# Expert stages: most token tiles dense on TensorE, the rest fetched row by row on VectorE

## The reference

```python
def block(hb):                       # 128 tokens
    q = (hb @ wq).reshape(n, 8, 2, 128)
    s = jnp.einsum('thpk,hpnk->thpn', q, keys)
    s1, i1 = lax.top_k(s[:, :, 0], 16)
    s2, i2 = lax.top_k(s[:, :, 1], 16)
    cand = (s1[..., :, None] + s2[..., None, :]).reshape(n, 8, 256)
    cidx = (i1[..., :, None] * 128 + i2[..., None, :]).reshape(n, 8, 256)
    sc, pos = lax.top_k(cand, 16)
    eidx = jnp.take_along_axis(cidx, pos, axis=-1)
    gw = jax.nn.softmax(sc, axis=-1)
    a = jnp.einsum('thkd,td->thk', u_tab[eidx], hb)
    w = gelu(a) * gw
    return jnp.einsum('thk,thkd->td', w, v_tab[eidx])
```

## Time and profile before

| | us |
|---|---|
| median of 3 runs | 5842.98 (5840.63 to 5846.96) |
| profiled execution, its own time | 5849.18 |
| its span, first to last instruction | 5847.3 |
| expert stage of layer 0 (from 1142.6 to 3329.3) | 2186.7 |
| expert stage of layer 1 (from 4334.9 to 5812.0) | 1477.1 |
| DVE busy | 4668.5 |
| PE busy | 1702.9 |

### The profile page before, as it was taken

One profiled execution on the slowest core, in us unless ns is written; L12 is line 12 of the kernel. 1 busy time (PEld: TensorE's weight loads), 2 busy tenths in 40 slices (PEclk: granted clock), 3 DMA queues, 4 the chain that ended last, 5 costly groups with the idle time before them and its releaser, 6 DMA issues. The chain is left out here.

```text
span 5847.3 us, 35407 instructions
## 1 busy us (share of the span) xinstructions
PE 1702.9 (29%) x9845; PEld 1288.3 (22%) x9845; DVE 4668.5 (80%) x7565; ACT 706.3 (12%) x993; POOL 2711.6 (46%) x2768
## 2 busy tenths in 40 slices
PE   6976888700000000000000087577750000000001
PEld 5844876600000000000000054333540000000001
DVE  3156753299999999999999925799339999999998
ACT  2134222100000000000000114444210000000000
POOL 0001320055676676767777400254006667677764
PEclk8987988855555555555555588888875555555555
DMA  4111012178999999999999710111219899999996
GB/s 153 51 59 62 5 30 80 66 312 316 358 407 387 365 406 345 409 370 375 409 410 409 283 39 1 39 47 44 78 67 366 321 355 410 368 376 409 409 410 279
DMA packets 477618, 1473.74 MB, mean 252 GB/s; under 512 B 55510, under 2 KB 124876, under 8 KB 474860
## 3 DMA queue, kind: packets, MB, share of 16 engines
q0 software_dynamic: 368640, 1342.34, 59.0%
q1 hardware_dynamic: 104336, 120.65, 6.3%
q10 hardware_dynamic: 4444, 8.48, 0.4%
HBM read 1458.72 MB, written 12.58 MB: 252 GB/s over the span
## 5 line engine op out<-in xcount | busy, mean ns | idle before, releaser
L1436 POOL DMA_INDIRECT rows<-peer_u,expert x1280 | 1224.0, 956 | 1261.7 <-DVE expert L1583 707.2
L1638 DVE SCALAR_TENSOR_TENSOR banks<-rows,weight,banks 128x1024 f32<-128x1024 f32 x1260 | 1534.8, 1285 | 5.8 <-DMA rows<-peer_v,expert 5.7
L1632 DVE CUSTOM_DVE_ANT_0 junk<-rows,banks 128x1024 f32<-128x1024 f32 x1280 | 1497.8, 1220 | 30.9 <-DMA rows<-peer_u,expert 18.4
L1436 POOL DMA_INDIRECT rows<-peer_v,expert x1280 | 1208.1, 944 | 461.1 <-issue 228.9
L1457 PE MATMUL banks<-ident,y_tok 128*128 128x128 f32 x80 | 19.7, 427 | 3088.8 <-DVE y_tok L1601 3088.8
L1457 PEld LDWEIGHTS banks<-ident,y_tok 128*128 128x128 f32 x80 | 15.7, 223 | 3091.5 <-DVE y_tok L1601 3091.5
L2169 POOL TENSOR_TENSOR prods<-s,cos 128x512 f32<-128x512 f32 x64 | 81.0, 1265 | 607.2 <-DVEq L2154 607.2
L1009 POOL TENSOR_TENSOR z<-expo,keep_k 128x384 f32<-128x384 f32 x28 | 30.8, 1107 | 606.5 <-ACT expo L985 606.5
L1483 ACT COPY y_tok<-banks 128x1024 f32<-128x1024 f32 x10 | 10.1, 1012 | 1576.7 <-DVEq L1654 1576.7
L1450 PE MATMUL banks<-ident_r,h_hi 128*128 128x128 f32 x80 | 33.6, 420 | 528.5 <-DVEq L1654 515.3
L1473 ACT ACTIVATE gate<-gate 128x128 f32<-128x128 f32 x10 | 3.1, 310 | 1342.0 <-DVE gate L1561 1342.0
(11 more groups left out here) (378 smaller groups left out, 5409.4 us busy)
## 6 DMA issues: line engine op xcount, KB each, us to landing
rows<-peer_u,expert POOLq DMA_INDIRECT x1280, 9.4
rows<-peer_v,expert POOLq DMA_INDIRECT x1280, 10.1
peer_wq_in<-peer_wq SPq DMA_DIRECT2D x16, 1024.0 KB, 5.3
ada_ring<-ada_w SPq DMA_DIRECT2D x32, 512.0 KB, 3.8
y_t<-ev_w_in SPq DMA_DIRECT2D x12, 1024.0 KB, 5.3
ada_ring<-ada_w SPq DMA_DIRECT2D x6, 2048.0 KB, 8.0
scores<-score_out SPq DMA_DIRECT2D x10, 1024.0 KB, 3.9
score<-scores SPq DMA_DIRECT2D x10, 1024.0 KB, 7.9
```

Source lines behind the costliest of these rows:

```text
L1436: pool.indirect_dma_start(out=ring[:, at % RING, :], out_offset=None, in_=tables[kind == "v"], in_offset=bass.IndirectOffsetOnAxis(ap=expe ...
L1632: last = nc.vector.tensor_tensor_reduce(out=junk[:, s % 2], in0=row, in1=tile_h(t), scale=1.0, scalar=0.0, op0=ALU.mult, op1=ALU.add, accu ...
L1638: last = nc.vector.scalar_tensor_tensor(out=acc(s % 2), in0=row, scalar=weight[:, t, s:s + 1], in1=acc(s % 2), op0=ALU.mult, op1=ALU.add)
```

## The change

The expert stage becomes two stages, and each token tile is now of one of two kinds. Layer 0 has four dense tiles and two fetched ones, layer 1 three and one (`DENSE_TILES`).

For **dense tiles** all 16384 experts are evaluated. `stage_peer_activate` goes over 128 expert tiles of 128 rows of `peer_u` (expert = 128 a + b; tile b holds the rows with the same b, so a partition reads 4 KB at a stride of 512 KB). For each, ACT makes the high part `u_hi` (`round_u`), POOL the low part `u_lo` (`low`), PE turns both by 16 transposes in two halves, ACT copies the turned halves out of PSUM (`turned_out`), PE makes 24 products of 512 (layer 1: 384) token columns, ACT applies gelu, and SP stores the result in HBM (`activations`). The gates of a dense tile become a table in HBM as well: for four tokens at a time (`quad`) DVE makes one-hot matrices (`one_hots`: one 128x512 comparison and four 128x128 operations), PE multiplies them, ACT copies the result (`keep`). `stage_peer_mix` reads `peer_v`, the activations and the gate table back, in 32 groups of 4 expert tiles: DVE multiplies activations by gates (`multiply`), ACT and DVE split the product (`w_hi`, `low`), ACT and POOL split `v` (`v_hi`, `v_lo`), and PE sums 12 products for each of 8 channel blocks; DVE adds each to the residual (`add`).

For **fetched tiles** nothing changes in kind: 256 fetches and dot products in the first stage of layer 0 and 256 fetches and weighted sums in the second (layer 1: 128 and 128), now with a ring of 8. They and the routing are spread over the expert tiles by a table of row numbers (class `Turns`, whose constants set the expert tile in which a gate event stands in the lists of PE, ACT and SP, and in which POOL fetches). The score stage also stores the residual in HBM (3 MB), since its room in SBUF is used for the routing, and the second stage loads it again. The total of fetches falls from 2560 to 768; 256 MB of tables are read in order.

```diff
+RING = 8
+DENSE_TILES = (4, 3)
...
+            self.events.setdefault(min(self.expert_tile(row) + 1, KEYS), []).append((kind, i))
...
+    def us(self, row):
+        steps = min(max(row, 0), (len(self.order) - 1) * 32)
+        return 60 + 1.4 * min(row, self.rows) + 1.9 * steps + 2.0 * self.quads_before(row)
+
+    def expert_tile(self, row):
+        return int(self.us(row) / self.tile_us)
...
+            def load(i):
+                if i >= 2:
+                    sp.wait_ge(u_lo_ready, i - 1)
+                sp.dma_start(u_raw[:, i % 2:i % 2 + 1], u_rows[:, i:i + 1, :]).then_inc(u_loaded[i % 2], 16)
...
+            def low(i):
+                pool.wait_ge(u_hi_ready, i + 1)
+                nc.gpsimd.tensor_tensor(u_lo[:, i % 2], u_raw[:, i % 2], u_hi[:, i % 2].bitcast(F32), ALU.subtract)\
+                    .then_inc(u_lo_ready, 1)
...
+            for i in range(KEYS):
+                if i + 2 < KEYS:
+                    low(i + 2)
+                while s < plan.rows and plan.expert_tile(s - 4) <= i:
+                    fetch(s)
+                    s += 1
...
+            def turn(i, half):
+                if half == 0:
+                    pe.wait_ge(u_lo_ready, i + 1)
+                if i or half:
+                    pe.wait_ge(ut_ready, 2 * i + half)
+                for at, u in ((TURN_HI, u_hi), (TURN_LO, u_lo)):
+                    for k in range(HALF):
+                        c = (half * HALF + k) * P
+                        last = nc.tensor.transpose(ps[:, at + k * P:at + (k + 1) * P].bitcast(F32R),
+                                                   u[:, i % 2, c:c + P], ident_r[:])
+                last.then_inc(turned, 1)
...
+            def products(i, half):
+                pe.wait_ge(ut_ready, 2 * i + half + 1)
+                if half == 0 and i >= 2:
+                    pe.wait_ge(gelued, i - 1)
+                out = ps[:, ACTS + i % 2 * BANK:ACTS + i % 2 * BANK + ND]
+                for k in range(half * HALF, (half + 1) * HALF):
+                    for u, h in ((ut_hi, hi), (ut_hi, lo), (ut_lo, hi)):
+                        last = nc.tensor.matmul(out, u[:, i % 2, k * P:(k + 1) * P], h[:, k, 0:ND],
+                                                start=(k == 0 and u is ut_hi and h is hi),
+                                                stop=(k == DK - 1 and u is ut_lo))
+                if half:
+                    last.then_inc(acted, 1)
...
+            def round_u(i):
+                act.wait_ge(u_loaded[i % 2], 16 * (i // 2 + 1))
+                if i >= 2:
+                    act.wait_ge(turned, 2 * (i - 2) + 2)
+                nc.scalar.copy(u_hi[:, i % 2], u_raw[:, i % 2]).then_inc(u_hi_ready, 1)
+
+            def turned_out(i, half):
+                act.wait_ge(turned, 2 * i + half + 1)
+                if i >= 2:
+                    act.wait_ge(acted, i - 1)
+                c = half * HALF * P
+                nc.scalar.copy(ut_hi[:, i % 2, c:c + BANK], ps[:, TURN_HI:TURN_HI + BANK])
+                nc.scalar.copy(ut_lo[:, i % 2, c:c + BANK], ps[:, TURN_LO:TURN_LO + BANK]).then_inc(ut_ready, 1)
+
...
+            for i in range(KEYS):
+                if i:
+                    gelu(i - 1)
+                if i + 2 < KEYS:
+                    round_u(i + 2)
+                if i + 1 < KEYS:
+                    turned_out(i + 1, 0)
+                keep(due(i))
+                if i + 1 < KEYS:
+                    turned_out(i + 1, 1)
+                if i == 8:
+                    soft(0)
+                if i in softs:
+                    soft(softs[i])
+            gelu(KEYS - 1)
+            keep(due(KEYS))
+            act.wait_ge(consumed, plan.rows)
...
+            def one_hots(q):
+                b = q % HOTS
+                if q % (P // QUAD) == 0:
+                    dve.wait_ge(kept, plan.at["slots", q // (P // QUAD)] + 1)
+                if q >= HOTS:
+                    dve.wait_ge(multiplied, plan.at["quad", q - HOTS] + 1)
+                c = q * QUAD
+                nc.vector.tensor_tensor(first_hot[:, b], iota[:].unsqueeze(1).to_broadcast([P, QUAD, P]),
+                                        slots[:, 0, c:c + QUAD].unsqueeze(2).to_broadcast([P, QUAD, P]),
+                                        ALU.is_equal)
+                for j in range(QUAD):
+                    last = nc.vector.tensor_scalar(gate_hot[:, b, j], iota[:], slots[:, 1, c + j:c + j + 1],
+                                                   slots[:, 2, c + j:c + j + 1], ALU.is_equal, ALU.mult)
+                last.then_inc(hot_ready, 1)
...
+                    if i:
+                        sp.wait_ge(v_lo_ready, at + r - GROUP + 1)
+                    sp.dma_start(v_raw[:, r:r + 1], v_rows[:, at + r:at + r + 1, :]).then_inc(v_loaded[r], 16)
+                    j = at + r
+                    if j >= ACT_ROWS:
+                        sp.wait_ge(w_lo_ready, j - ACT_ROWS + 1)
+                    sp.dma_start(acts[:, j % ACT_ROWS], acts_d[j]).then_inc(acts_loaded[j % ACT_ROWS], 16)
+                    if r == 0:
+                        if i >= 2:
+                            sp.wait_ge(weighted, (i - 1) * GROUP)
+                        sp.dma_start(gates[:, i % 2], table[:, :, at:at + GROUP, :])\
+                            .then_inc(gates_loaded[i % 2], 16)
+                if i == 0:
+                    sp.dma_start(g.x_t[:], x_d).then_inc(x_loaded, 16)
...
+            for j in range(KEYS):
+                i, r = divmod(j, GROUP)
+                pool.wait_ge(v_hi_ready, j + 1)
+                nc.gpsimd.tensor_tensor(v_lo[:, i % 2, r], v_raw[:, r], v_hi[:, i % 2, r].bitcast(F32), ALU.subtract)\
+                    .then_inc(v_lo_ready, 1)
+                while s < plan.rows and s < (j - 3) * PER // GROUP + RING - 2:
+                    fetch(s)
...
+            for j in range(KEYS):
+                i, r = divmod(j, GROUP)
+                act.wait_ge(v_loaded[r], 16 * (i + 1))
+                if r == 0 and i >= 2:
+                    act.wait_ge(y_done, (i - 1) * DK)
+                nc.scalar.copy(v_hi[:, i % 2, r], v_raw[:, r]).then_inc(v_hi_ready, 1)
+                act.wait_ge(weighted, j + 1)
+                nc.scalar.copy(w_hi[:, i % 2, r], acts[:, j % ACT_ROWS]).then_inc(w_hi_ready, 1)
...
+            for i in range(GROUPS):
+                for m in range(DK):
+                    u = i * DK + m
+                    if u >= BANKS:
+                        pe.wait_ge(y_added, u - BANKS + 1)
+                    out = ps[:, u % BANKS * BANK:u % BANKS * BANK + ND]
+                    for r in range(GROUP):
+                        if m == 0:
+                            pe.wait_ge(v_lo_ready, i * GROUP + r + 1)
+                            pe.wait_ge(w_lo_ready, i * GROUP + r + 1)
+                        for v, w in ((v_hi, w_hi), (v_hi, w_lo), (v_lo, w_hi)):
+                            last = nc.tensor.matmul(out, v[:, i % 2, r, m * P:(m + 1) * P], w[:, i % 2, r],
+                                                    start=(r == 0 and v is v_hi and w is w_hi),
+                                                    stop=(r == GROUP - 1 and v is v_lo))
+                    last.then_inc(y_done, 1)
...
+            def multiply(j):
+                i, r = divmod(j, GROUP)
+                dve.wait_ge(acts_loaded[j % ACT_ROWS], 16 * (j // ACT_ROWS + 1))
+                if r == 0:
+                    dve.wait_ge(gates_loaded[i % 2], 16 * (i // 2 + 1))
+                x = acts[:, j % ACT_ROWS].rearrange("p (b t) -> p b t", t=TB)
+                nc.vector.tensor_tensor(x, x, gates[:, i % 2, :, r, :], ALU.mult).then_inc(weighted, 1)
...
+            dve.wait_ge(x_loaded, 16)
+            for i in range(GROUPS):
+                for m in range(DK):
+                    u = i * DK + m
+                    for s in range(u * PER // DK, (u + 1) * PER // DK):
+                        weighted_row(s)
+                    if i + 1 < GROUPS:
+                        if m < GROUP:
+                            multiply((i + 1) * GROUP + m)
+                        else:
+                            low((i + 1) * GROUP + m - GROUP)
+                    if u:
+                        add(u - 1)
+            add(GROUPS * DK - 1)
```

More of the change, by code:

```diff
@@ L1377, in stage_peer_gather, with stage_peer_activate @@
+def stage_peer_activate(nc, g, layer, hi, lo, scores_d, acts_d, table, plan, expert, weight):
+    NT, G2, ND, NG = plan.tiles, 2 * PEER_H, plan.dense * P, plan.fetched
+    rows_of_u = g.d["peer_u"].rearrange("l e d -> (l e) d")
+    u_rows = g.d["peer_u"][layer].rearrange("(a b) d -> a b d", b=KEYS)
+    HALF = DK // 2
     with ExitStack() as stack:
         a = Arena(nc, stack)
-        score = a.sb("score", [P, G2, P])
-        rest = a.sb("rest", [P, G2, P])
-        cand = a.sb("cand", [P, PEER_H, TOPK * TOPK])
@@ new lines, in soft @@
+            def soft(rank):
+                act.wait_ge(soft_in, rank + 1)
+                t = plan.order[rank]
```

(32 more changed lines are left out.)

495 lines of the change are left out of this document (333 added, 162 removed).

## The result

The changed kernel takes 5754.48 us (median of 4 runs, 5736.15 to 5761.88) beside 5841.81 us for the kernel before in the same session: a ratio of 0.984, 95% interval 0.9827 to 0.9854. It is 87 us (1.6%) faster, which is clear of the noise but less than 2%; the forecast was 5600, 244 faster. The profiled execution of after is its fastest, 5736.15 with a span of 5734.3, so traces compare as 5847.3 to 5734.3, 113 us.

The account below looks back on a forecast made before the run. Taking one DVE operation and one transfer per fetched row as the bound, it summed the new stages to 1050 + 861 + 888 + 612 + 9 = 3420 us for 3663.8, so 5843 - 244 = 5600 us, range 5430 to 5820.

Parts of the forecast that it names:

- Prices of TensorE: Activate stages: an expert tile's products, transposes and gate quad take 7.89 us in layer 0, 6.44 in layer 1.
- layer 0's mix stage: DVE's `multiply` waits for POOL's `v_lo`, making a group 27 us and the stage 888 us.
- In layer 1 ... only half of the steps hold a row, so 18.5.: Layer 1's mix stage: DVE has slack against collisions, so a group takes 18.5 us and the stage 612.
- rival 2: Mix stages: full collision at each `multiply`, groups of 29.4 and 22.2 us, 195 us more, 5795 us; chance 0.14.
- For waits at the hand-offs I add 2%: Activate stages: 2% for hand-off waits, plus 20 us for first loads and drained end, giving 1050 and 861 us.
- Rival 3: Activate stages: slower hand-off between TensorE and ACT, with 1.2 us per expert tile 5907 us; chance 0.09.
- its sign: Activate stages: PE waiting for ACT above 5% of the time would show the slower hand-off.
- Layer 1 as a whole: Layer 1's two expert stages together: 861 us for activate and 612 for mix, against 1477.1 before.
- Rivals 4 and 5: TensorE's clock falls in the activate stages, 5924 us, chance 0.05; strided loads slow the mix stages, 5984 us, chance 0.05.
- sign given for rival 5: DVE and ACT waiting for `u_raw` or `v_raw` would show that strided loads are slow.
- 8-in-10 range: Whole kernel: 5430 to 5820 us, said to leave out the lower half of rival 1 and all slower cases but one.
- rival 1: Mix stages: no collision between DVE and POOL, groups of 22.5 and 17.4 us, 179 us less, 5420 us; chance 0.16.

Follow-up runs that it names:

- e3: Changed kernel with its mix stages in two phases, so DVE's two-input operations and POOL's `v_lo` cannot meet, all computation kept; 5519.31 us, 0.9447 of the kernel before.
- e5: Changed kernel with the second input of DVE's `multiply` and `low` in the mix stages taken from PSUM, gates and low parts left out; 5494.12 us (one run).
- e4: Changed kernel with SP issuing each `u` load one tile earlier in the activate stages; 5666.92 us, 0.9698 of the kernel before.
- e1: Changed kernel with layer 1 put back to the gather stage of before, layer 0 staying changed; 5623.73 us, 0.9625 of the kernel before.

## Why the prediction was off

The direction, the bounds (TensorE in the activate stages, DVE in the mix stages) and the clock (0.95 to 0.98 in all four) were right, and the time lay in the range. The gain was not: 87 us for 244. Two terms of the sum were too small, the waits at the hand-offs in the activate stages and the group of layer 1's mix stage. The sum, with 9 us for boundaries, was 3420 and came out at 3559: 34 and 49 more in the activate stages, 71 more in layer 1's mix stage, 6 less in layer 0's, and 9 less for the boundaries, which the windows already hold. The other stages gave 9 back. The last 26 us of the 157 are spread: the profiled execution of after lies 18 us under its median, that of before 7 over. By the prediction's own steps:

- *Prices of TensorE, and layer 0's mix stage.* Tiles of 7.90 us for 7.89, groups of 26.4 us for 27: right, and the mechanism of the mix stages was the one named, read rightly. e3 and e5 show it: 143 and 140 us in layer 0. That 27 came so near is in part luck. It holds no stall on `low`, which was 1.8 us a group, and it puts DVE's own work at 21.8 us, where e5 shows 20.3 (busy 279.3 of 300 us, at 21.8 us a group); the records of successive operations overlap by some 0.08 us each.
- *"In layer 1 ... only half of the steps hold a row, so 18.5."* This step failed: 20.3 us, 73 us over the stage, of which some 8 are a later start (first product at 5033.9, 20.3 us behind the cut in the table, for 12). I put the stall on `multiply` and expected `low` near its own time. But `low` is of the same kind: 1.02 us of stall on each `low`, 0.90 on each `multiply`. About as many were held as in layer 0 (58 and 67 of 128, against 61 and 64), but a held `low` lost 2.2 us where in layer 0 it lost 1.0, since 33 of the 58 opened at most 0.5 us into the subtraction, or ahead of it as in the meeting shown above, for 4 of 61 in layer 0. The slack that I gave DVE in layer 1 was time in which it stood held, and TensorE waited for the late `w_lo` (89.5 us with the start) more than for additions (25.1). The truth lay half way to rival 2 (22.2).
- *"For waits at the hand-offs I add 2%".* This step failed too: 51 us in layer 0 and 87 in layer 1 for 20 and 17. Rival 3 named the place, a late `u` load that holds ACT and then TensorE, and set it at 0.09 because there are two buffers of each; its sign, TensorE waiting for ACT above 5% of the time, just showed in layer 1 (48.5 us for `ut_lo`, 5.3%). That both buffers were tied to SP's order wasn't worked out: a load stood behind the store that waits for `gelu`, which left it one tile, 7.9 us in layer 0 but 5.6 to 6.5 in layer 1, against 5.3 to land and 12.2 behind a gate table store. e4, which only moves the load, gives 84 us back. The 26 and 28 us that are left after e4 were not tested. One candidate is in the trace of after: the meetings occur here too. 20 `first_hot` and 26 `gate_hot` lie held beside a `u_lo`, up to 2.90 us, and 23 `u_lo` are themselves long, 17 us in all. In layer 1 the tiles themselves came out 23 us under their price (821 for 844 with the start), which hid a third of this.
- *Layer 1 as a whole* was forecast at no gain, so every missed microsecond there was a loss; e1 shows 131 us.
- *Rivals 4 and 5* didn't come: no stage fell under 0.95, and no load pace of strided pieces shows (383 GB/s in e5 with them). The sign given for rival 5, ACT waiting for `u_raw`, did show, but e4 removed it with the pieces as they were.
- *The chances.* "Faster" had 0.85 and "same" 0.03; where a change counts only from 2% on, 1.6% is "same". And the 8-in-10 range, by its own terms, leaves out 0.08 of rival 1 and 0.19 of rivals 3 to 5, so it held nearer 0.73.
